# Masking the delta rule's system matrix on GpSimd ahead of its levels, with a plain ScalarE copy in place of VectorE's masking pass

## The reference

```python
kk = jnp.einsum('bhtk,bhsk->bhts', k, k)
a_strict = jnp.tril(beta[..., :, None] * decay * kk, -1)
rhs = beta[..., None] * (v - eG[..., None] * jnp.einsum('bhtk,bhkv->bhtv', k, S))
u = lax.linalg.triangular_solve(a_strict, rhs, left_side=True, lower=True, unit_diagonal=True)
```

## Time and profile before

| what | value |
|---|---|
| median of 3 runs | 4484.14 us (4483.48 to 4489.67) |
| the profiled execution | 4486.8 us, its span 4485.0 us |
| PE / PEld busy | 2377.1 (53%) / 1882.1 us (42%) |
| DVE busy | 3309.7 us (74%), 4373 instructions |
| ACT busy | 588.3 us (13%) |
| POOL busy | 2318.3 us (52%), 1217 instructions |
| HBM read and written | 1384.96 and 126.21 MB, 337 GB/s over the span |
| gathers by GpSimd's queue | 1158.85 MB, 63.6% of the 16 engines' span |

### The profile page before, as it was taken

How to read it: one execution, slowest core, us unless ns; L and a number is a source line. 1 busy time by engine, 2 the same in 40 slices (tenths; PEclk the granted TensorE clock), 3 DMA queues, 4 the chain that set the end, 5 groups by cost and what they waited for, 6 DMA issues and landing times. The chain is left out here.

```text
span 4485.0 us, 35227 instructions
## 1 busy us (share of the span) xinstructions
PE 2377.1 (53%) x11697; PEld 1882.1 (42%) x11697; DVE 3309.7 (74%) x4373; ACT 588.3 (13%) x1450; POOL 2318.3 (52%) x1217
## 2 busy tenths in 40 slices
PE   6999999898488899888849774100000000000000
PEld 5888888787366666666637553000000000000000
DVE  2333323305769999989886788999998989999998
ACT  1222222301112222222210010000000000000000
POOL 1011010000235566645664412788887888888886
PEclk8999999899789999999969887555555555555555
DMA  6766666396769999999999965899999999999998
GB/s 176 224 206 204 188 204 196 126 325 226 256 271 396 402 416 400 406 369 414 366 405 405 386 225 177 359 422 422 419 422 397 421 413 422 419 418 419 409 420 352
DMA packets 444573, 1513.70 MB, mean 338 GB/s; under 512 B 42684, under 2 KB 276848, under 8 KB 278488
## 3 DMA queue, kind: packets, MB, share of 16 engines
q0 software_dynamic: 161840, 1158.85, 63.6%
q1 hardware_dynamic: 269880, 251.94, 17.6%
q10 hardware_dynamic: 12672, 100.67, 5.6%
HBM read 1384.96 MB, written 126.21 MB: 337 GB/s over the span
## 5 line engine op out<-in xcount | busy, mean ns | idle before, releaser
L1958 DVE SCALAR_TENSOR_TENSOR ex_y<-ex_ring,ex_wt,ex_y 128x2048 f32<-128x2048 f32 x538 | 1264.6, 2351 | 98.6 <-DMA ex_ring<-in_peer_v_dram,idx_all 54.0
L1943 DVE CUSTOM_DVE_ANT_0 ex_ring<-ex_ring,ex_xi 128x2048 f32<-128x2048 f32 x544 | 1244.6, 2290 | 114.6 <-DMA ex_ring<-in_peer_u_dram,ex_idx_s 46.8
L1865 POOL DMA_INDIRECT ex_ring<-in_peer_v_dram,idx_all x384 | 809.8, 2109 | 260.5 <-DVE ex_y L1958 145.3
L1865 POOL DMA_INDIRECT ex_ring<-in_peer_u_dram,idx_all x384 | 781.8, 2036 | 280.9 <-DVE ex_hid L1943 170.1
L1897 PE MATMUL ex_fold<-ex_y,const 128*32 128x512 f32 (+1 forms) x48 | 25.8, 705 | 1110.7 <-DVE ex_y L1958 1110.7
L863 PE MATMUL heads_b_pj<-xnT_b,lead 128*128 128x304 f32 x2048 | 604.0, 433 | 7.2 <-PEq L285 3.6
L1897 PEld LDWEIGHTS ex_fold<-ex_y,const 128*32 128x32 f32 (+1 forms) x48 | 6.6, 141 | 1129.5 <-DVE ex_y L1958 1112.0
L1865 POOL DMA_INDIRECT ex_ring<-in_peer_v_dram,ex_idx_s x160 | 300.8, 1880 | 283.8 <-DVE ex_y L1958 200.7
L863 PEld LDWEIGHTS heads_b_pj<-xnT_b,lead 128*128 128x128 f32 x2048 | 376.2, 196 | 119.3 <-issue 16.3
L1865 POOL DMA_INDIRECT ex_ring<-in_peer_u_dram,ex_idx_s x160 | 314.9, 1968 | 193.1 <-DVE ex_hid L1943 147.5
L863 PE MATMUL heads_a_pj<-xnT_a,heads_a_w 128*128 128x256 f32 x1216 | 316.2, 398 | 1.7 <-DMA heads_a_w<-in_w_in_dram 1.7
(11 more groups left out here) (585 smaller groups left out, 3986.9 us busy)
## 6 DMA issues: line engine op xcount, KB each, us to landing
lead<-w_scratch SPq DMA_DIRECT2D x64, 1024.0 KB, 9.1
heads_a_w<-in_w_in_dram SPq DMA_DIRECT2D x38, 1024.0 KB, 6.0
w_scratch<-heads_a_w ACTq DMA_DIRECT2D x38, 1024.0 KB, 4.1
lead<-in_w_in_dram SPq DMA_DIRECT2D x26, 1024.0 KB, 5.8
w_scratch<-lead ACTq DMA_DIRECT2D x26, 1024.0 KB, 4.1
out_a_w<-in_w_out_dram SPq DMA_DIRECT2D x7, 2048.0 KB, 14.4
w_out_scratch<-out_a_w ACTq DMA_DIRECT2D x7, 2048.0 KB, 9.3
out_b_w<-w_out_scratch SPq DMA_DIRECT2D x7, 2048.0 KB, 12.8
```

The lines of the kernel that those rows point to most:

```text
L1865: pool.indirect_dma_start(self.ring[:, i % RING, :], None, self.tables[which], bass.IndirectOffsetOnAxis(ap=self.index(s, g, k), axis=0)). ...
L1943: nc.vector.tensor_tensor_reduce(ring, ring, self.tokens(s)[:], 1.0, 0.0, ALU.mult, ALU.add, self.hid[:, g % 2, k:k + 1]).then_inc(self.se ...
L1958: nc.vector.scalar_tensor_tensor(y, ring, wt, y, ALU.mult, ALU.add).then_inc(self.sem["consumed"], 1)
```

## The change

The masks are applied to `A` instead of to the product. GpSimd gets a new generator `parts()`: for each head and level it multiplies `A` by `mask_l` (no longer transposed) into `part[l % 2]`, which lies in `th_root`, and raises `A_masked`. Level 1 waits for `A_ready`; from the third on each waits for `QT_done` of two levels earlier. L954 now multiplies `part[l % 2]` instead of `A`, and waits for `A_masked`. R1 then already holds QT, and ScalarE copies it (`QT_copied`) at the mark where VectorE had masked it. In the second group GpSimd's gathers are no longer one list: `gathers()` yields at each item's mark + 0.02 and issues those of that step, and `Marks` interleaves the parts. The exponential that writes `EN` of the next head waits for `A_masked` of the last.

```diff
-        "levels": np.concatenate(levels[:1] + [m.T for m in levels[1:]], 1),
+        "levels": np.concatenate(levels, 1),
...
+               part=th_root[:, 0:2 * TW].rearrange("p (s t c) -> p s t c", s=2, t=T), sq=buf["qke"], A=buf["EN"], oN=buf["gU"],
...
+    def item_mark(i):
+
+        return (100.0 * HEADS + 50) * (i + 0.5) / quota
...
                         pe.wait_ge(sem["XT_ready"], h * (LV + 1) + l)
+                        pe.wait_ge(sem["A_masked"], h * LV + l)
                         for t in range(T):
-                            last = nc.tensor.matmul(R1[:, t * P:(t + 1) * P], B.A[:, t, :], B.XT[:, t, :], start=True, stop=True)
+                            last = nc.tensor.matmul(R1[:, t * P:(t + 1) * P], B.part[:, l % 2, t, :], B.XT[:, t, :],
+                                                    start=True, stop=True)
                         last.then_inc(sem["QT_done"], 1)
                         yield at + 33.5 + 8 * (l - 1)
-                        pe.wait_ge(sem["QT_masked"], h * LV + l)
+                        pe.wait_ge(sem["QT_copied"], h * LV + l)
...
                     act.wait_ge(sem["decay_done"], n)
+                    if h > 0:
+                        act.wait_ge(sem["A_masked"], h * LV)
...
+                    for l in range(1, LV + 1):
+                        yield at + 32 + 8 * (l - 1)
+                        act.wait_ge(sem["QT_done"], h * LV + l)
+                        nc.scalar.copy(wide(B.QT), R1[:, 0:TW]).then_inc(sem["QT_copied"], 1)
...
                     for l in range(1, LV + 1):
-                        yield at + 32 + 8 * (l - 1)
-                        dve.wait_ge(sem["QT_done"], h * LV + l)
-                        nc.vector.tensor_tensor(B.QT[:], tiles(R1), cst("levels", l * P, (l + 1) * P).unsqueeze(1)
-                                                .to_broadcast([P, T, P]), ALU.mult).then_inc(sem["QT_masked"], 1)
...
+            def parts():
+
+                for h in range(HEADS):
+                    for l in range(1, LV + 1):
+                        yield 100.0 * h + (26 + 0.5 * l if l < 3 else 31 + 8 * (l - 3))
+                        if l == 1:
+                            pool.wait_ge(sem["A_ready"], h + 1)
+                        if h * LV + l > 2:
+                            pool.wait_ge(sem["QT_done"], h * LV + l - 2)
+                        nc.gpsimd.tensor_tensor(B.part[:, l % 2], B.A[:], cst("levels", l * P, (l + 1) * P).unsqueeze(1)
+                                                .to_broadcast([P, T, P]), ALU.mult).then_inc(sem["A_masked"], 1)
+
+            def gathers():
+                for i in range(quota):
+                    yield item_mark(i) + 0.02
+                    share.gather_to(pool, i + 1)
...
             if samples:
-                Marks(gdn(), fox()).run()
+                Marks(gdn(), fox(), parts()).run()
...
+            else:
+                Marks(parts(), gathers()).run()
             share.gather(pool)
...
+    def gather_to(self, pool, step):
+
+        if self.stream:
+            self.stream.gather(pool, self.at(step))
```

More of the change, by code:

```diff
@@ L612, in heads @@
         "decayT_exp upto_exp decay_exp tails_exp convolved tanh_y silu_done squared squares_done root_q root_k inverted "
-        "qk_ready grown gate_ready tanh_z v_turned v_copied k_turned kN_ready kk_done qk_done A_ready PT_ready "
-        "X_ready XT_turned XT_ready QT_done QT_masked Y_done YT_done "
+        "qk_ready grown gate_ready tanh_z v_turned v_copied k_turned kN_ready kk_done qk_done A_ready A_masked PT_ready "
+        "X_ready XT_turned XT_ready QT_done QT_copied Y_done YT_done "
         "grown_apart ks_done w_ready u_done u_copied um_ready ds_done S_ready o_done "
@@ L652, in heads @@
     buf.update(th=th_root[:, 0:3 * N].rearrange("p (s c) -> p s c", s=3),
-               root=th_root[:, 0:2 * TW].rearrange("p (s c) -> p s c", s=2), sq=buf["qke"], A=buf["EN"], oN=buf["gU"],
+               root=th_root[:, 0:2 * TW].rearrange("p (s c) -> p s c", s=2),
+               part=th_root[:, 0:2 * TW].rearrange("p (s t c) -> p s t c", s=2, t=T), sq=buf["qke"], A=buf["EN"], oN=buf["gU"],
                y=yX[:, :, 0:N], X=yX[:, 0, :].rearrange("p (t c) -> p t c", t=T),
@@ L1350, in gelus @@
                     share.gelu(act, i + 1)
-            def item_mark(i):
-                return (100.0 * HEADS + 50) * (i + 0.5) / quota
             act.wait_ge(sem["f_cleared"], 5)
@@ L1362, in items @@
                 for i in range(quota):
-                    yield (100.0 * HEADS + 50) * (i + 0.5) / quota
+                    yield item_mark(i)
                     share.take(dve, i + 1)
```

## The result

The kernel before had a median of 4489.7 us beside the changed one's 4511.2 us: a ratio of 1.0050 (95% interval 1.0037 to 1.0062), or 22 us. The profiled run of the changed kernel took 4515.2 us with a span of 4513.5 us, that of before 4486.8 and 4485.0.

The account below looks back on a forecast made before the run. TensorE sets the pace in heads_a; in heads_b VectorE, TensorE and DMA are all near their limit. Terms 0 (heads_a) + 3 (VectorE) + 7 (late first parts) = +10 us on the 4484.1 median: forecast 4494 us, range 4464 to 4518.

Parts of the forecast that it names:

- `heads_a`, 0 (-1 to +4): First group's head stage: TensorE sets the pace, so VectorE's saved 20.4 us buy nothing; 0, bounds -1 to +4 us.
- VectorE in `heads_b`, +3: Second group's head stage: passes removed -26.4, blocks by GpSimd products +32.0, idle time -2.5; +3 us, bounds -26.4 to +19.
- the later one blocks: SBUF rule in `heads_b`: of a two-input VectorE operation and a GpSimd one reading SBUF, the later waits fully; 40 x 0.80 us.
- Rival B: `heads_b` is bound by the gathers' DMA; VectorE's +3 or -5 us vanish in waits for landings; 4484 us, chance 0.32.
- Rival A: Masking really leaves VectorE in `heads_b`, products slip into gaps if blocks are under about 0.4 us; -16 us, 4468, chance 0.23.
- Late first parts, +7 (0 to 43): `heads_b`: mask 1 queues behind delayed gathers, holding TensorE and then VectorE; 5 + 3 x 0.7 = +7 us, bounds 0 to 43.
- rival C: GpSimd becomes the bound in `heads_b`: masks cost each head two turns or the ring runs empty; 4523 us, chance 0.10.
- (1): `heads_a` keeps its length within 4 us, with TensorE's waits there under 10 us each.
- (2): GpSimd's mask rows take 0.7 to 0.95 us where VectorE is idle, up to 3 us in items.
- (3): VectorE in `heads_b`: L1481 gone, some 35 to 40 items near 3.1 us instead of 2.3, busy time about equal.
- (4): TensorE's L954 gets a new wait for GpSimd, a few us in heads with a long gather.
- (5): From the end of `heads_b` to the end of the kernel nothing changes but the shift.

Follow-up runs that it names:

- level1_unwaited: Changed kernel, but level 1 multiplies A itself without waiting for GpSimd (adds nothing); all products still run: +14 us (9 to 19) against the kernel before.
- no_masks: Changed kernel without GpSimd's products; VectorE's pass also gone, ScalarE's copies stay, scaled by zero: +3 us (-2 to +9) against the kernel before.
- gpsimd_1_2: Changed kernel with GpSimd and ScalarE taking levels 1 and 2 only, VectorE masking levels 3 to 6 as before: +16 us (9 to 22) against before.
- memset_parts: Changed kernel with each GpSimd product replaced by a memset to zero, same waits and turns, no SBUF reads: +1 us (-3 to +6) against before.
- twice_3_6: Changed kernel with the second group's products of levels 3 to 6 done twice, 32 more: ratio 1.0101, +45 us against before.

## Why the prediction was right in sign and short in size

The forecast was +10 us, the result +22: slower, inside the range, with VectorE's term too small. By the runs `heads_a` is +3.5 us against 0; what the products do in `heads_b` besides being late for level 1 is 10 to 14 us against +3 (level1_unwaited without `heads_a`, and its b); and the late first part is 4 to 8 against +7. So the shortfall lies in the second, not in the third. Of the 17 us between the forecast 4494 and the measured 4511.2, 5.5 are the kernel before itself (4484.1 in the three runs shown, 4489.7 in five).

**`heads_a`, 0 (-1 to +4).** Measured +3.5, at the end of the bound. I had looked at GpSimd's first product; it was ScalarE's copy, which I had called free because the view of waits showed no wait for the old pass.

**VectorE in `heads_b`, +3.** Its busy time rose by 2.9 us in the two windows and by 5.9 us over equal work (b), so the match to the number is luck. The parts were not these. The product takes 1.016 us, above my 0.80 and above the 0.94 of my upper bound; the 256-element one takes 0.731. Instead of 40 blocks of 0.80 us (32 us) there are 22 long items with 24.9 us. The pass removed gave less as well: 18.4 us of busy time in b for 42 passes (no_masks), or 21 for all 48, not 26.4. The first step behind this held only in part: I had each product wait for an item to end, one operation of GpSimd per item. 22 of 48 do, and end about 0.86 us behind it; the other 26 take 1.0 us, twice in a row inside one item four times, and there it is the item that stands. It stands even where it began up to 0.44 us ahead of the product, so by the profile's starts my "the later one blocks" isn't the rule. The rest of the shortfall is in waits for rows: in level1_unwaited VectorE is 7.3 us busier in b than before and stands 10.6 us longer for rows. I had written that gathers 3 or 6 us later change little in quiet heads. That the rows are late because their gathers stand behind the products is likely, and no run shows it apart.

The more instructive error is the sign that I gave the -26.4: I set a pass removed and a block added against each other as if both were worth their time. no_masks shows the pass at +3 (-2 to +9) us instead of -26.4, and level1_unwaited shows the blocks at +14 with the pass gone: in b, against no_masks, VectorE is 25.7 us busier and b is 13.7 us longer, so about half of that counts. A cut in a stage that is fed by the DMA goes into waits for rows; of the blocks only a part does. Rival B said the first half of this ("disappear in its waits for landings"), and applied it to both halves. Rival A needed blocks under 0.4 us, and they are 1.04.

**Late first parts, +7 (0 to 43).** In time this term came out near: the wait for the first part alone is worth 4 to 8 us (level1_unwaited). (All that the products of levels 1 and 2 do costs 16, gpsimd_1_2.) In waits it was too small. The mechanism was the one described: a long gather, a backlog, a product behind it, TensorE's wait, which is 16.0 us in five heads. I had one such head with 5 us and three with 0.7; it was five, of 3.2 us each on average. Four of them come 21 to 22 us after the start of a gather of 6.1 or 6.5 us, and wait 3.3 to 4.3 us; the fifth has no gather over 3.6 us ahead of it and waits 1.5. For three heads I had priced a lag of 2.4 to 3.8 us at 0.7 us each, as if TensorE's other matmuls and the ring took up the rest. TensorE's waits were larger than that, and a half or less of them reached the time: without them VectorE stands longer for rows instead (47.0 us against 34.4). That the sum came near +7 is so in part luck. And I had VectorE held at L1485 by L960 behind L954. It was held two operations earlier in its own order, at L1618 by L1161, the other branch's matmul: 15.1 us. I had looked at who needs L954, not at **who stands behind it in TensorE's queue**.

**GpSimd as the bound (rival C).** No. memset_parts keeps every turn of GpSimd and costs 1 us. But there isn't much room for longer ones: in twice_3_6, 32 products more cost 23 us, and VectorE stands 14.7 us longer for rows.

**What would show it.** Of the five signs (1) held but for TensorE's waits being no guide to a 3.5 us loss; (2) was low on the short ones (1.0 us, not 0.7 to 0.95) and right on the long (up to 3.04); (3) held in part, with 22 items and not 35 to 40, of 2.7 to 4.8 us, and a busy time 5.9 us up; (4) held, and was larger; (5) held as far as it can be told: that stretch scatters by 10 us.

No version tried with the full weight loads is faster than the kernel before. Even no_masks and memset_parts, in which nothing is masked, only equal it; so on this kernel as it stands there was nothing to win by moving this mask off VectorE with a ScalarE copy in its place.

## What to carry over

Before a pass is moved off a busy engine, take it away altogether and time that: here it was worth nothing, and with that nothing was left to win by moving it. A GpSimd product of 1.0 us that reads SBUF and starts with a two-input operation of VectorE costs VectorE its whole length here; one that starts later in it waits for its end. And when an engine works in order, a wait put in front of one matmul delays the unrelated work behind it: look at the queue, not only at the data's users.

## What was not expected of the hardware

- GpSimd's products take 0.731 us for 256 elements a partition, 1.016 us for 384, 1.26 us for 512 and 1.90 us for 1024. 128 elements more cost 0.285, 0.24 and then 0.16 us each, so neither a price per element nor one straight line fits. My bounds scaled each row by its elements alone, down to 0.71 and 0.94 us; a line through the two rows would have given 1.10 us, and the truth lay between.
- An operation of VectorE that reads one tensor from SBUF and a column was held too, which my "and no other" had ruled out. L1979 of the changed kernel takes 1.29 us as a rule and 2.12 us once, beside a product of 1.01 us that began at 1349.41 us:

```profile
1349.40 2.12 DVE L1979 TENSOR_SCALAR ex_y<-ex_ring,ex_wt 128x2048 f32<-128x2048 f32 x1 [0.80 <-DMA ex_ring<-in_peer_v_dram,idx_all]
```

- Some gathers take 6.0 to 6.5 us, where the others of `heads_b` take 0.9 to 3.7, also in no_masks (five in `heads_b`, as before), and no run here shows why. They are behind four of the five late first products.
